# Moving a norm's channel factors from the weights to the transposed input, with constant products ahead of the first load and input transposes between pieces of the first weight block

## The reference

```python
def rmsnorm(x, g):
    y = x32 * lax.rsqrt(jnp.mean(x32 * x32, axis=-1, keepdims=True) + EPS)
    return (y * g.astype(jnp.float32)).astype(x.dtype)

h = rmsnorm(x, norm_mix_g)
z = h @ w_in          # w_in: 1024 x 5640
u_pool, u_ssm, q, k, v, logf, gates = columns of z
...                   # pooling mixer, state-space mixer, forgetting attention
x = x + (merged @ w_out)
x = x + conv_ffn(rmsnorm(x, norm_ffn_g), ...)
```

## Time and profile before

| | |
|---|---|
| median of 3 runs | 1763.65 us (1763.05 to 1763.67) |
| profiled execution, its own time | 1760.58 us |
| its span, first to last instruction | 1758.8 us |
| TensorE busy | 1726.5 us, 98% |
| VectorE, GpSimd, ScalarE busy | 1208.8, 678.6, 642.9 us |
| TensorE busy in the first 20 us | 14.65 us |

### The profile page before, as it was taken

One profiled execution on the slowest core, in us unless ns is written; L12 is line 12 of the kernel. 1 busy time (PEld: TensorE's weight loads), 2 busy tenths in 40 slices (PEclk: granted clock), 3 DMA queues, 4 the chain that ended last, 5 costly groups with the idle time before them and its releaser, 6 DMA issues.

```text
span 1758.8 us, 31148 instructions
## 1 busy us (share of the span) xinstructions
PE 1726.5 (98%) x12335; PEld 1658.5 (94%) x12335; DVE 1208.8 (69%) x1881; ACT 642.9 (37%) x1231; POOL 678.6 (39%) x473
## 2 busy tenths in 40 slices
PE   8999999999998999999999999999999999999997
PEld 8999999888888889989999999999999999999997
DVE  5888563566664567553574688877777777798685
ACT  6210013555551222250012445444444444534343
POOL 4654334334356667422333224544455554000000
PEclk9999999999999999999999999999999999999999
DMA  8634728675735554456545332222222221998252
GB/s 280 201 121 133 232 101 253 172 186 151 185 94 156 129 124 93 98 184 240 188 146 171 99 92 74 74 75 74 74 74 74 79 86 58 371 340 273 90 194 89
DMA packets 246755, 260.69 MB, mean 148 GB/s; under 512 B 50161, under 2 KB 198365, under 8 KB 246162
## 3 DMA queue, kind: packets, MB, share of 16 engines
q1 hardware_dynamic: 232482, 227.49, 43.2%
q10 hardware_dynamic: 14128, 31.21, 5.0%
HBM read 178.09 MB, written 76.09 MB: 145 GB/s over the span
## 4 chain that ended last, share of the span: by engine, by line
PE 53%; DVE 6%; POOL 3%; DMA 3%; ACT 1%; issue 1%; SPq 0%; ACTq 0%; DVEq 0%; POOLq 0%
PE bank L156 50%; DMA down_raw<-in_w_down 1%; DMA gate<-gate_scratch 1%; DVE merged L2301 1%; PE bank L2018 1%; PE bank L1975 1%; POOL w_lo L872 1%; POOL w_raw L868 1%; DVE prod L2294 1%; POOL ssm_wt L1712 1%; POOL ssm_w L1715 1%; POOL ssm_w L1710 0%; PE bank L2003 0%; POOL w_hi L870 0%; DVE xt L3130 0%
## 5 line engine op out<-in xcount | busy, mean ns | idle before, releaser
L156 PE MATMUL bank<-act_hi,w_hi 128*128 128x364 f32 (+1 forms) x1296 | 435.8, 336 | 5.9 <-POOL w_lo L872 1.6
L156 PE MATMUL bank<-act_lo,w_hi 128*128 128x364 f32 (+1 forms) x1296 | 425.6, 328 | 0.0
L156 PE MATMUL bank<-act_hi,w_lo 128*128 128x364 f32 (+1 forms) x1296 | 425.4, 328 | 0.0
L156 PEld LDWEIGHTS bank<-act_hi,w_hi 128*128 128x128 f32 x1296 | 243.7, 188 | 16.4 <-issue 6.3
L156 PE MATMUL bank<-x_forms,up_forms 128*128 128x272 f32 x1824 | 254.9, 289 | 1.0 <-DVE up_raw L3198 0.8
L156 PEld LDWEIGHTS bank<-act_lo,w_hi 128*128 128x128 f32 x1296 | 243.7, 188 | 0.1
L156 PEld LDWEIGHTS bank<-act_hi,w_lo 128*128 128x128 f32 x1296 | 243.2, 188 | 0.0
L156 PEld LDWEIGHTS bank<-x_forms,up_forms 128*128 128x128 f32 x1824 | 239.1, 188 | 1.7 <-DVE up_forms L3192 1.0
L156 PE MATMUL bank<-act_form,down_form 128*128 128x272 f32 x1848 | 233.4, 288 | 1.8 <-DVE y_t L3316 1.2
L156 PEld LDWEIGHTS bank<-act_form,down_form 128*128 128x128 f32 x1848 | 231.6, 188 | 2.7 <-DVE y_t L3316 1.7
L2676 POOL TENSOR_TENSOR up_forms<-up_w_raw,up_forms 128x512 fp32r<-128x512 f32 x60 | 89.1, 1485 | 185.7 <-ACT up_forms L2929 185.7
(11 more groups left out here) (392 smaller groups left out, 2957.6 us busy)
## 6 DMA issues: line engine op xcount, KB each, us to landing
down_raw<-in_w_down SPq DMA_DIRECT2D x121, 256.0 KB, 4.5
w_raw<-in_w_in SPq DMA_DIRECT2D x44, 512.0 KB, 4.8
up_w_raw<-in_w_up SPq DMA_DIRECT2D x44, 512.0 KB, 4.7
gate<-gate_scratch ACTq DMA_DIRECT2D x24, 544.0 KB, 4.0
act_scratch<-ffn_act SPq DMA_DIRECT2D x22, 544.0 KB, 4.8
act_raw<-act_scratch SPq DMA_DIRECT2D x44, 272.0 KB, 4.8
gate_scratch<-gate_out ACTq DMA_DIRECT2D x48, 182.0 KB, 2.5
w_raw<-in_w_out SPq DMA_DIRECT2D x14, 512.0 KB, 4.3
```

Of the source, the lines that this page charges most:

```text
L156: mm = pe.matmul(out, w(k), x(k)[:, c0:c0 + cn], start=first and k == ks[0] and n == 0, stop=last and k == ks[-1] and n == 2, skip_group_c ...
```

## The change

The gain is taken off the weights everywhere: `split_tile`, the entry's loop, attention's `scale`, the gates of the mixing stage and the forget columns lose the multiplication and its semaphore. Instead VectorE multiplies the transposed input by the gain as it takes it out of PSUM, half by half, into one of two SBUF buffers (`gained`); ScalarE rounds a whole tile from there to the high part (`x_high`) and VectorE subtracts for the low part (`x_low`), each written one tile behind the multiplication. ScalarE's copy of half b waits for VectorE's multiplication of half b. TensorE multiplies a tile of ones by itself four times before the gain's transpose and three times after it. The transposes of tiles 4 to 7 stand between quarters of group 0 of block 0.

```diff
-def split_tile(pool, m, s, a, n, gain=None):
-    if gain is not None:
-        pool.tensor_tensor(m.raw[:, a], m.raw[:, a], gain, ALU.mult).then_inc(s.w_scaled, 1)
-        pool.wait_ge(s.w_scaled, n + 1)
+def split_tile(pool, m, s, a, n):
     pool.tensor_copy(m.wh[:, a], m.raw[:, a]).then_inc(s.w_hi, 1)
...
+        gained = (dve_sq, z[:, 1, 0:D])
+        xg = lambda j: gained[j % 2].rearrange("p (k c) -> p k c", c=P)[:, :, 0:TOK[j][1]]
...
         def gpsimd(pool):
-            pool.wait_ge(g_out, 1)
-            gain = by_channel(m.gain1[:])
             for t in range(len(TILES)):
                 a = t % 2
                 pool.wait_ge(w_ld[a], 16 * (t // 2) + 16)
                 if t == 1:
                     pool.wait_ge(x_lo, 6)
-                pool.tensor_tensor(m.raw[:, a], m.raw[:, a], gain, ALU.mult).then_inc(w_scaled, 1)
...
         def tensor(pe):
+            def occupy(times):
+                for _ in range(times):
+                    pe.matmul(acc[1][:, 2, 0:P], m.ones[:], m.ones[:], start=True, stop=True)
+
             pe.wait_ge(const, 5)
+            occupy(4)
             pe.wait_ge(g_ld, 16)
             pe.transpose(acc[0][:, 0, 0:KD], grow[:], m.ident[0:KD, 0:KD]).then_inc(g_turned, 1)
+            occupy(3)
...
-                    pe.wait_ge(x_lo, before + 1)
+                    pe.wait_ge(x_gain, 2 * before + 2)
                     pe.wait_ge(x_out, before + 1)
...
-            for j in range(5):
+            for j in range(4):
                 turn_x(j)
             pe.wait_ge(w_split, 1)
             pe.wait_ge(x_lo, 3)
-            for q in range(2):
-                group(0, 0, 0, range(4 * q, 4 * q + 4))
-                turn_x(5 + q)
-            turn_x(7)
+            for q in range(4):
+                group(0, 0, 0, range(2 * q, 2 * q + 2))
+                turn_x(4 + q)
...
         def scalar(act):
+            def x_high(j):
+                cols = slice(TOK[j][0], TOK[j][0] + TOK[j][1])
+                act.wait_ge(x_gain, 2 * j + 2)
+                act.activation(m.hh[:, :, cols], xg(j), ACT.Copy).then_inc(x_hi, 1)
...
                 act.activation(xr[:, half_a, cols], x[:, half_a, 0:cn], ACT.Copy).then_inc(x_out_a, 1)
-                act.activation(m.hh[:, half_b, cols], x[:, half_b, 0:cn], ACT.Copy)
+                act.wait_ge(x_gain, 2 * j + 1)
                 act.activation(xr[:, half_b, cols], x[:, half_b, 0:cn], ACT.Copy).then_inc(x_out, 1)
+                if j:
+                    x_high(j - 1)
                 if j in (4, 5):
                     square(j - 4)
+            x_high(8)
...
         def vector(dve):
+            def x_low(j):
+                cols = slice(TOK[j][0], TOK[j][0] + TOK[j][1])
+                dve.wait_ge(x_hi, j + 1)
+                dve.tensor_tensor(m.hl[:, :, cols], xg(j), m.hh[:, :, cols].bitcast(F32), ALU.subtract
+                                  ).then_inc(x_lo, 1)
+
             for j, (c0, cn) in enumerate(TOK):
                 x, cols = by_k[home[j]], slice(c0, c0 + cn)
+                gain = m.gain1[:].unsqueeze(2).to_broadcast([P, KD, cn])
+                dve.wait_ge(x_turned, j + 1)
+                if j > 1:
+                    dve.wait_ge(x_lo, j - 1)
+                dve.tensor_tensor(xg(j)[:, half_b], x[:, half_b, 0:cn], gain[:, half_b], ALU.mult).then_inc(x_gain, 1)
                 dve.wait_ge(x_out_a, j + 1)
-                dve.tensor_copy(m.hh[:, half_a, cols], x[:, half_a, 0:cn]).then_inc(x_hi, 1)
-                dve.wait_ge(x_hi, j + 1)
-                dve.tensor_tensor(m.hl[:, half_a, cols], x[:, half_a, 0:cn], m.hh[:, half_a, cols].bitcast(F32), ALU.subtract)
-                dve.wait_ge(x_out, j + 1)
-                dve.tensor_tensor(m.hl[:, half_b, cols], x[:, half_b, 0:cn], m.hh[:, half_b, cols].bitcast(F32), ALU.subtract
-                                  ).then_inc(x_lo, 1)
+                dve.tensor_tensor(xg(j)[:, half_a], x[:, half_a, 0:cn], gain[:, half_a], ALU.mult).then_inc(x_gain, 1)
+                if j:
+                    x_low(j - 1)
+            x_low(8)
...
             low(("q", 1))
             dve.wait_ge(wf_ld, 16)
-            dve.tensor_tensor(wf[:], wf[:], m.gain1[:].unsqueeze(2).to_broadcast([P, KD, HEADS]), ALU.mult).then_inc(wf_scaled, 1)
             slot(2)
```

38 lines of the change are left out of this document (14 added, 24 removed).

## The result

The changed kernel takes 1776.77 us in the median (1776.05 to 1779.24, six runs), the kernel before, run beside it, 1763.21 (1761.76 to 1763.67, six runs): a ratio of 1.0080 with a 95% interval of 1.0070 to 1.0091, or 12.3 to 16.0 us more. The forecast was 1778.5, with 1772 to 1784 as its range and slower as its sign. The profiled execution took 1776.29 us by its own time, 1.8 over its span, against 1760.58 before: 15.7 us more.

The account below looks back on a forecast made before the run. TensorE, busy 1726.5 of 1758.8 us, was taken as the bound, so only its waits or lower clock count. Head +16.5 and mixing start -1.6 gave +14.9 on 1763.65: 1778.5 us, range 1772 to 1784.

Parts of the forecast that it names:

- ring per tile: Head: VectorE and ScalarE wait for each other in turn through their in-order queues, 3.47 us per token tile.
- first products: Head, TensorE: block 0 starts once the third low part is there, at 19.5 us instead of 13.87.
- third group, with a fall of the clock: Head, TensorE: block 0's third token group starts 14.7 us later, 16.5 with group 0 at 1.2 GHz.
- the falls: Head: TensorE idles from about 12 to 19.5 us, so group 0 starts at 1.2 GHz; 1.8 us.
- constants: Start of head: seven ones-tile products on TensorE may raise the clock earlier or delay the first transposes; taken as zero.
- scalings in the projections: Projections: removing GpSimd's weight scalings gains nothing, since they lay in its 106.1 us wait for TensorE.
- scalings in attention: Attention: transposes wait 2.0 us for VectorE; removing scalings could win between 0 and 2.0 us; taken as 0.
- scalings at the start of mixing: Mixing stage's start: TensorE's two waits for low parts made behind scalings both go, -1.6 us.
- the mark: Start of block 0's third token group on TensorE, 25.67 us before; expected between 39 and 43 after.
- rival of a lower level throughout: Head: TensorE stays at the lower clock until the first block's end; +17.3 us, 1781.0; chance 0.14.
- The hold by GpSimd: Head: GpSimd's work on weight block 1 holds VectorE's low part of tile 6 until 35.5 us, +1.2.
- The open ring: Rival, head: engines run at their own rates, 2.35 us per tile, third group at 29.7; +2.4 us, 1766.0; chance 0.08.

Follow-up runs that it names:

- e6: Changed kernel plus 32 and 16 more products of the ones tile in TensorE's two long gaps, to hold the clock up; 1777.95 us, 1.0089 to before.
- e2: Changed kernel without the seven products of the ones tile at its start; 1776.47 us, 1.0080 to before.
- e4: Kernel before with only the seven products of the ones tile added; 1763.91 us, 1.0008 to before.
- e5: Kernel before with the scalings of weights by the first norm's channel factors removed and nothing in their place; 1759.73 us, 0.9982 to before.
- e9: Kernel before with the scaling of the mixing stage's first two weight blocks moved to GpSimd's idle time at attention's end; 1760.21 us, 0.9991 to before.
- e1: Changed kernel with ScalarE rounding the previous tile's high part before it copies half b; 1773.31 us, 1.0065 to before.
- e8: Changed kernel with ScalarE's high part before its copy, the old transpose order, and 16 ones-tile products before the first products; 1767.05 us, 1.0026 to before.
- e11: e8 with GpSimd's second weight block started behind the ninth low part, and 8 ones-tile products before the wait for the sixth; 1767.90 us, 1.0030 to before.

## Why the prediction held, step by step

| step | predicted | measured |
|---|---|---|
| ring per tile | 3.47 us | 3.63 us |
| first products | 19.5 us | 20.16 us |
| third group, with a fall of the clock | 25.67 + 16.5 | 25.67 + 17.75 |
| of that, the falls | 1.8 us, one fall | 1.8 to 2.6 us, two falls (e6) |
| constants | 0 | 0 (e2), -0.3 in the kernel before (e4) |
| scalings in the projections | 0 | -0.8 us (e5: -0.7) |
| scalings in attention | 0 | 0 (-0.1) us; up to -0.8 not excluded (e9) |
| scalings at the start of mixing | -1.6 us | -2.0 us (e5 and e9 too) |
| sum, to the median and in the traces | +14.9 us | +13.6, and +15.7 |

**The ring** was right in its mechanism, and e1 shows it: a change of order in one engine's queue, with the same work, brings 5.6 us at the mark. Its size was 0.16 us short, in one link. The step from the subtraction's start to the next multiply was priced at 1.13 us, with the overlap of VectorE's ends that the earlier trace rows show between its steps; it measures 1.34, because this multiply itself waits for a subtraction's signal (line 1424) and so doesn't start before the last one has ended. The other three links came to 2.29 against 2.34.

**First products**: 0.66 late, 0.3 from the two turns of the ring and the rest from GpSimd's first block, which ended at 11.7 instead of 11.2 us as its load landed later in this execution.

**The clock** was expected to fall once before the first products; it fell twice. The prediction had counted three gaps (7, 5 and 4 us) and let the level fall only in the first. The second low stretch covers all of group 1, and at 43.42 group 1's last product and the last low part (it ends at 43.37) come together; e6 shows what the stretch cost, 0.3 us, through tile 8's transposes. The rival of a lower level throughout didn't come: the level rose at 23.3 us. In e2, without constants, sixteen transposes from 4.62 take 3.51 us with weight loads of 227 ns, as where the clock reads 0.50 (230 ns from 21.4 us in the same trace), and the eight from 9.01 take 1.09 with 141 ns, as at the upper level; the granted clock reads 1.00 in both places, so at the start it is the durations that tell the level. Nothing but transposes ran between. The sentence cited from the Trainium skill (TensorE: Matmul & The Clock Gate, Part 4: PE-mode transpose), that transposes don't count as activity, does not hold in these rows.

**The hold by GpSimd** was placed on the low part of tile 6 at 1.2 us; it is 1.07 (2.30 against 1.23).

**Downstream** the step that failed is "in the projections nobody waited for them": it looked at GpSimd's waits alone. TensorE's transposes at line 1193 of the kernel before wait 0.6 us for VectorE's copies there, in e4 and e9 too, and in neither the changed kernel nor e5. Ahead of those copies VectorE's subtraction that GpSimd holds up takes 2.72 or 2.73 us in the three kernels with scalings and 2.12 in the changed kernel and e5: the same 0.6 us. The 2.0 us in which attention's transposes wait for VectorE stayed in the changed kernel, as the prediction had taken it. At the mixing stage 2.0 instead of 1.6 went.

**The sum** hit partly by cancelling: the head was 1.5 us worse (at the spread), the rest up to the first Toeplitz product 1.2 better, and 0.6 went behind it, where the last stage varies by itself. The mark, at 43.42, lies just above the 39 to 43 named as a sign. Of the 1.25 us that it was short of, 0.4 stand at tile 4's multiply (23.79 against 21.6 + 1.8), 0.5 are three turns of the ring, 0.44 the wait for tile 8, and the hold gave 0.1 back. The median's 13.6 and the traces' 15.7 both lie in the interval's 12.3 to 16.0; the profiled execution of before lay 2.6 us under the median of its runs, that of after 0.5 under.

**The open ring** as a rival had been priced at 2.35 us per tile and a third group at 29.7. Opened (e1, e8), a tile cost 2.53 at best and 2.9 with a square in ScalarE's queue, and the mark stood at 33.87 even with the clock held (32.66 in e11, without GpSimd's hold). The prediction's "The two squares in ScalarE's queue fit into its ring gaps" is true only of the closed ring, whose gaps they fill; the rival's price left them out, and the hold with them.

## What to carry to other kernels

When a change puts a new step between two in-order engines, write each engine's queue beside the other's and add the links from one step back to itself: the largest closed sum is the price of a tile, whatever the busy shares say; here the second buffer didn't lower it. Before replacing work on an idle engine by work on the engines that feed the bound, ask which few of the removed instructions anyone waited for; here two of 44 held 2.0 of the 2.7 us, and they could be moved. Behind a wait that is removed or filled, price the next one in line first: here it was the squares, GpSimd's second block and the clock in turn.
